# Three products of a recurrent stage rewritten: E by an identity, the decay in one product, the keys' norm by a block of ones

## The chip, the cores and the metric

The kernel runs on one core of one Trainium2 chip. The metric is the device time of one execution in microseconds; shown are the median of three runs and their ends. The program computes a whole network of eight layers in float32; the change touches one stage of it, a recurrent mixer that takes some 700 of its 3980 us.

## The reference, cut to what matters

The stage computes `rwkv_mixer` for 768 time steps (256 of a context, 512 of the sequence) and 16 heads of 64 channels, in two directions:

```python
kk = heads(k * k_k)
kk = kk * lax.rsqrt(jnp.sum(kk * kk, axis=-1, keepdims=True) + 1e-12)      # the keys' norm, per head and step
...
def step(S, inp):
    d_t, k_t, v_t, kk_t, a_t = inp[:5]
    sa = jnp.einsum("bhvk,bhk->bhv", S, -kk_t)
    S = (S * d_t[:, :, None, :] + sa[..., None] * (kk_t * a_t)[:, :, None, :]
         + v_t[..., None] * k_t[:, :, None, :])
    out = jnp.einsum("bhvk,bhk->bhv", S, inp[5])
    return S, out
```

`S` is a 64x64 state for each head, `d_t` the decay of each channel.

## The kernel before

The program is written engine by engine with explicit semaphores: the order of the text is the order on each queue, nothing is reordered. TensorE's products all carry the line of one helper (L1029), ScalarE's functions L1994, and most fused products of VectorE L2589, so the trace is read by tiles and shapes.

**Chunks and groups.** Two heads share the 128 partitions (64 each). There are 8 blocks of two heads (`j`), each with 12 chunks of 64 steps; a group `G` takes 4 chunks in both directions, 8 units in all, so a block is 3 groups (`G % 3` is 0, 1, 2) and there are 24 groups. Inside a chunk the recurrence is a triangular system. Its inverse is built by doubling: E and its transpose F start from the identity (`start_e` L3213, `start_f` L3219 copy the part of a product of features that lies next to the diagonal into it, under a mask) and grow in levels 1 to 5. A level `l` is one round over three engines:

- TensorE `level_z` (L1646; with products of the features of this or the next group in between, L1653): z of 8 units, from `nq` and F
- ScalarE `take_z` (L2372): copies z out of PSUM
- TensorE `level_fz_ez` (L1688): two products a unit, with E (level 5 has only one of the two)
- VectorE `level_f` (L3225) and `level_e` (L3230): copies under a mask; TensorE's next `level_z` waits for `level_f`.

A product of 64x64 is made for each of the two heads, on one quarter of the array each: `heads` (L1504) writes a head's result to its own 64 partitions, `crossed` (L1510) to the other's. One float32 matmul of the program is two weight loads and two products in the trace.

**The chain of states.** Beside the levels of group G the state goes through the 4 chunks of group G-1: `chain_xo` (L1738), `chain_u` (L1759) and `chain_m` (L1765) on TensorE. `chain_m` adds up the new state in PSUM: the old state, multiplied by an identity on each half (`turn`, L1776), and two products. A state step at the first chunk of a block has no old state, the one at the last is left out, so 80 of the 96 steps multiply by the identity.

**E's first product.** `ends(G)` (L1616) is 16 matmuls: features B times features A, crossed, for 8 units, into `qe_ps` (L640), a bank of its own use. It stands in level 3 of the group before, between `chain_xo` and `level_fz_ez` (L1825). `nq` (L2364) is ScalarE's copy of the same features' product, the other way round, made in levels 4 and 5 by `take_b` after VectorE's `mask_b` (L3240).

**The keys' norm.** For block j+1 the work is spread over the levels of block j's first two groups, by the tables `aside` (L1781 for TensorE, L2403 for ScalarE, L3316 for VectorE): ScalarE squares the keys (L2297), TensorE sums the squares of each head for every step, as 6 matmuls with 2 columns of ones (`key_sums` L1519), ScalarE takes the root of 128x12 values (L2316), VectorE its reciprocal (L3190), and TensorE spreads the result over the 64 channels of each head in 12 matmuls (`key_spread` L1528, levels 4 and 5). VectorE multiplies the keys by it out of PSUM in `keys` (L3197): 512 steps in level 4 of the block's first group, 256 in level 1 of its second. GpSimd makes the features A, B, K, R of the block from them (L3609 on); TensorE waits for these features in level 3 of the third group. `read_gains` (L2310, ScalarE) writes the reads' gains into the buffer `bon`, in which the squares stood, and GpSimd goes on from there to the bonus.

**The bonus.** `bonus_sums` (L1540) writes into `spare_ps`, which is the bank of `level_fz_ez`'s first product, in level 5 of each third group; VectorE's `bonus_values` (L3205) reads it behind `level_e`. TensorE waits for that in level 1 of the next group (L1694).

**Before the loop** the rates of all 8 blocks come from matmuls (`lora_up` L1487) whose results ScalarE evicts (`lora_rates` L2289); the keys of block 0 are prepared between those of blocks 1 and 2 (L1796 to L1803, L2433 to L2451).

Of the kernel before, what the change touches and what calls it, by code (L numbers as in the profile page):

```python
# [13 lines left out]
P = 128  # L14
# [150 lines left out]
CHUNK = 64  # L165
# [97 lines left out]
def build(nc, t):  # L263
# [27 lines left out]
    with ExitStack() as ctx:  # L291
# [348 lines left out]
        qe_ps, qt_ps = [lin_ps[:, 0, 512 * i:512 * i + 512].rearrange("p (u t) -> p u t", u=UN) for i in range(2)]  # L640
# [21 lines left out]

        def ends_job(G):

            return 6 * G + 2

        def b_job(G, half):

            return 6 * G + 3 + half

# [356 lines left out]
        def _(pe):  # L1027
# [488 lines left out]
            turn = C("twice")  # L1516
            pe.wait_ge(in_ready, 16 * (LOADS + 2))

            def key_sums(j):  # L1519

                pe.wait_ge(kk_sq, j + 1)
                if j:
                    pe.wait_ge(b_ev, 2 * j)
                for n in range(6):
                    m = mm(pair_ps[:, 2 * n:2 * n + 2], bon[:, n * P:(n + 1) * P], headones[:, 0:P:64], True, True)
                m.then_inc(kk_mm, 1)

            def key_spread(j, part):  # L1528

                if part == 0:  # L1530
                    pe.wait_ge(kk_inv, j + 1)
                else:
                    pe.wait_ge(kk_n, 4 * j + 2)
# [16 lines left out]
            def values(j, part):  # L1550

                if part == 0:
                    pe.wait_ge(value_in, 16 * (j + 1))
                    pe.wait_ge(kk_n, 4 * j + 4)
                else:
                    pe.wait_ge(v_ev, 2 * j + 1)
# [46 lines left out]
            def ready_b(G, half):  # L1603
# [3 lines left out]
                else:  # L1607
                    if G % 3 == 0:
                        pe.wait_ge(read_ready, G // 3 + 1)
                    pe.wait_ge(e_init, G + 1)  # L1610
# [77 lines left out]
            def level_fz_ez(G, l, chain=None):  # L1688

                pe.wait_ge(z_ev, 5 * G + l)  # L1690
                if l == 1:
                    pe.wait_ge(e_init, G + 1)
                    if G and G % 3 == 0:
# [2058 lines left out]
```

## Time and profile before

| | |
|---|---|
| median of 3 runs | 3981.12 us (3980.13 to 3982.87) |
| the profiled execution | 3980.35 us, its span 3978.5 us |
| granted TensorE clock, share | 0.989 |
| TensorE busy | 3769.9 us, 95% of the span |
| weight loads busy | 2778.7 us, 70% |
| VectorE, ScalarE, GpSimd busy | 2301.6, 887.9, 1162.7 us |
| the recurrent loop | 2240 to 2880 us of the span |

The span is the profiled execution from its first to its last instruction; the device time has some 2 us more. The busy time of matmuls is modelled at their ends, so two short products in a row leave no idle time between them though the array is not full. "Idle before" is the time that an engine stood still before a group of its instructions, and behind the arrow stands what ended it; "issue" is the case in which the engine waited for nothing that the profile shows. Times of rows in a timeline are microseconds from the span's start.

### The profile page before, as it was taken

How to read it: one execution, taken by the hardware profiler on the slowest of the kernel's cores; microseconds unless marked ns; L12 is line 12 of the kernel's file. 1: busy time of each engine (PE TensorE's matmuls, PEld its weight loads, DVE VectorE, ACT ScalarE, POOL GpSimd, SP SyncE). 2: the span in 40 equal slices, each digit the busy share in tenths (PEclk: the TensorE clock that was granted, in tenths of full speed). 3: DMA queues.
4: the chain of work that ended last, by engine and by line, in shares of the span. 5: the costliest groups of instructions: out<-in, count | busy, mean ns of one | idle time of the engine just before them, and what ended most of it. 6: DMA issues, size and time to landing. Idle time of an engine off the chain costs nothing.

```text
span 3978.5 us, 77183 instructions
## 1 busy us (share of the span) xinstructions
PE 3769.9 (95%) x33844; PEld 2778.7 (70%) x33844; DVE 2301.6 (58%) x3572; ACT 887.9 (22%) x1689; POOL 1162.7 (29%) x860
## 2 busy tenths in 40 slices
PE   8999999999999999999999788888799999999998
PEld 3588887758888855555555677777757888558445
DVE  4577725658564139934553456655416877662695
ACT  2311101010110020021112544444212222550102
POOL 0154444105445420001341422342013554103202
PEclk9999999999999999999999899999999999999999
DMA  2133223433442211111333411111202333211221
GB/s 80 54 138 139 97 93 125 172 116 128 148 148 85 75 53 50 38 40 64 111 111 103 160 51 45 40 36 36 82 16 77 103 117 97 76 38 56 74 64 53
DMA packets 196056, 336.93 MB, mean 85 GB/s; under 512 B 17040, under 2 KB 149136, under 8 KB 187280
## 3 DMA queue, kind: packets, MB, share of 16 engines
q1 hardware_dynamic: 192000, 321.59, 24.1%
q0 software_dynamic: 3728, 10.49, 1.0%
q8 instruction: 264, 4.33, 0.4%
q14 instruction: 64, 0.52, 0.0%
HBM read 285.91 MB, written 38.80 MB: 82 GB/s over the span
## 4 chain that ended last, share of the span: by engine, by line
PE 86%; DVE 7%; issue 5%; ACT 1%; DMA 1%; SPq 0%; POOL 0%; DVEq 0%; ACTq 0%
PE lin_ps L1029 64%; PE out_ps L1029 8%; PE sum_ps L1029 7%; PE lin_ps L1434 6%; DVE arena L2589 1%; PE sum_ps L1939 1%; DVE rstd L2576 1%; ACT arena L1994 1%; DVE arena L3228 0%; DVE hn L2589 0%; DMA features<-arena 0%; DVE xs L2584 0%; DMA arena<-pos 0%; PE sum_ps L1153 0%; DVE arena L3238 0%
## 5 line engine op out<-in xcount | busy, mean ns | idle before, releaser
L1029 PE MATMUL lin_ps<-hn,ring 128*128 128x256 f32 (+1 forms) x3520 | 1001.0, 441 | 8.2 <-DVE hn L2589 5.1
L1029 PEld LDWEIGHTS lin_ps<-hn,ring 128*128 128x128 f32 x3520 | 667.8, 190 | 316.8 <-issue 249.8
L1029 PE MATMUL lin_ps<-arena 64*64 64x64 f32 (+5 forms) x10032 | 737.7, 261 | 70.5 <-issue 37.3
L1029 PE MATMUL lin_ps<-arena,ring 128*128 128x256 f32 (+1 forms) x3200 | 771.8, 396 | 11.0 <-DVE arena L3057 9.4
L1029 PEld LDWEIGHTS lin_ps<-arena,ring 128*128 128x128 f32 x3200 | 610.2, 191 | 136.3 <-issue 54.3
L1029 PEld LDWEIGHTS lin_ps<-arena 64*64 64x64 f32 (+2 forms) x10032 | 549.8, 145 | 189.9 <-issue 113.8
L2589 DVE SCALAR_TENSOR_TENSOR arena<-arena,vec 128x512 f32<-128x512 f32 (+2 forms) x491 | 384.5, 857 | 1.1
L1994 ACT ACTIVATE arena<-lin_ps 128x512 f32<-128x512 f32 (+3 forms) x375 | 191.7, 525 | 775.9 <-PE lin_ps L1029 707.5
L3544 POOL TENSOR_TENSOR arena<-ring 128x512 f32<-128x512 f32 x67 | 89.8, 1341 | 895.4 <-PE lin_ps L1029 537.9
L1029 PE MATMUL sum_ps<-arena 64*64 64x64 f32 (+1 forms) x7180 | 311.5, 225 | 33.7 <-issue 28.5
L3544 POOL TENSOR_TENSOR ring<-ring 128x512 f32<-128x512 f32 x67 | 102.7, 1533 | 732.0 <-PE lin_ps L1029 428.7
L2589 DVE SCALAR_TENSOR_TENSOR arena<-arena,cs 128x512 f32<-128x512 f32 x280 | 294.8, 1108 | 1.8
L1029 PEld LDWEIGHTS sum_ps<-arena 64*64 64x64 f32 (+1 forms) x7180 | 257.1, 135 | 45.1 <-issue 34.6
L1994 ACT ACTIVATE xs<-lin_ps 128x256 f32<-128x256 f32 x88 | 33.6, 382 | 921.4 <-PE lin_ps L1029 921.4
L1029 PE MATMUL lin_ps<-hn,arena 128*128 128x256 f32 x928 | 214.5, 379 | 0.0
L1029 PEld LDWEIGHTS lin_ps<-hn,arena 128*128 128x128 f32 x928 | 176.3, 190 | 24.0
L1029 PE MATMUL out_ps<-arena 64*64 64x64 f32 (+3 forms) x2142 | 171.3, 254 | 4.4 <-issue 3.2
L2783 DVE TENSOR_TENSOR xs<-lin_ps,xs 128x256 f32<-128x256 f32 x24 | 10.1, 421 | 279.9 <-ACT xs L1994 279.8
L1029 PEld LDWEIGHTS out_ps<-arena 64*64 64x64 f32 (+1 forms) x2142 | 122.7, 143 | 46.4 <-issue 40.0
L1029 PE MATMUL sum_ps<-arena,con 64*64 64x64 f32 (+2 forms) x830 | 129.7, 305 | 21.1 <-ACT arena L1994 16.9
L1994 ACT ACTIVATE arena<-arena 128x512 f32<-128x512 f32 (+3 forms) x220 | 125.4, 626 | 98.6 <-DVE arena L2805 35.3
L3228 DVE COPY_PREDICATED arena<-arena,lin_ps 128x512 f32<-128x512 int32 x96 | 70.3, 732 | 127.2 <-issue 127.1
(279 smaller groups left out, 4918.7 us busy)
## 6 DMA issues: line engine op xcount, KB each, us to landing
ring<-w_up SPq DMA_DIRECT2D x32, 1024.0 KB, 5.9
ring<-w_down SPq DMA_DIRECT2D x32, 1024.0 KB, 5.2
arena<-w_mod SPq DMA_DIRECT2D x24, 1024.0 KB, 7.8
arena<-w_mod SPq DMA_DIRECT2D x12, 2048.0 KB, 7.5
features<-arena SPq DMA_DIRECT2D x64, 384.0 KB, 6.2
ring<-w_conv_in SPq DMA_DIRECT2D x16, 1024.0 KB, 5.7
ring<-w_attn SPq DMA_DIRECT2D x16, 1024.0 KB, 5.8
ring<-features SPq DMA_DIRECT2D x40, 384.0 KB, 3.1
```

The source lines that it names most:

```text
L1029: return pe.matmul(out, lhsT, rhs, start=start, stop=stop)
L1434: m = pe.matmul(wide_bank[bank], w[:, k, :], rhs[:, k, :], start=first and k == 0, stop=k == 3, skip_group_check=not first)
L1939: m = pe.transpose(sum_ps[:, 256 + b * P:256 + (b + 1) * P], probs[U % 3][:, b * P:(b + 1) * P], ident)
L1994: return nc.scalar.activation(out, in_, func, **kw)
L2576: o(nc.vector.reciprocal(last_cols(rstd, width), last_cols(std, width)))
L2589: return nc.vector.scalar_tensor_tensor(*a)
L2783: o(add(c11, quad_ps[0][:, hi_t], p1, ALU.add), ev)
L3228: nc.vector.copy_predicated(by_step(F_[G % 2]), level_mask(l, 1), by_step(fz_ps)).then_inc(f_ready, 1)
L3544: o(tt(s1, a21, a22, ALU.add), block)
```

## The change

Three products of the stage are made in another way, and two of them at another place.

1. E's first product: `ends(G)` is now one `crossed` product over all 8 units, of the identity with `nq` (2 matmuls of 512 columns in place of 16 of 64). It waits for `nq`'s second half, is written into `spare_ps`, and so waits for `bonus_values` where a new block starts. It moves from level 3 of the group before to behind its level 5; `start_e` moves with it on VectorE, behind `level_e` of level 5. The features' products of the next group wait for `f_init` in place of `e_init`.
2. The decay in `chain_m`: one matmul of the 128x128 identity with both directions' old state (128 columns) in place of 4 of 64x64.
3. The keys' norm: TensorE multiplies the squares by a 128x128 block of ones (`headones`), 512 and 256 columns, which gives each channel its head's sum; ScalarE takes the root of all these values into `bon`, VectorE the reciprocal of all of them in `keys`, and multiplies the keys by it out of SBUF. `key_inverse` and `key_spread` are gone. `read_gains` moves from level 1 to level 2 of the second group and waits for the keys.

```diff
+        def b_job(G, half):
+            return 6 * G + 2 + half
         def ends_job(G):
-            return 6 * G + 2
+            return 6 * G + 4
...
-            def key_sums(j):
-                ...
-                for n in range(6):
-                    m = mm(pair_ps[:, 2 * n:2 * n + 2], bon[:, n * P:(n + 1) * P], headones[:, 0:P:64], True, True)
-                m.then_inc(kk_mm, 1)
-            def key_spread(j, part):
...
-                for n in range(4 * part, 4 + 2 * part):
-                    lo = P * (n - 4 * part)
-                    for h, rows in enumerate(HALVES):
-                        m = mm(pair_ps[rows, lo:lo + P], kn[:, 1, 2 * n + h:2 * n + h + 1].to_broadcast([P, CHUNK]), ident, True, True)
-                m.then_inc(kk_bc, 1)
+            def key_sums(j, part):
+                if part:
+                    pe.wait_ge(kk_std, 2 * j + 1)
+                else:
+                    pe.wait_ge(kk_sq, j + 1)
+                    if j:
+                        pe.wait_ge(b_ev, 2 * j)
+                lo, n = (0, 512) if part == 0 else (512, 256)
+                mm(pair_ps[:, 0:n], headones, bon[:, lo:lo + n], True, True).then_inc(kk_mm, 1)
...
-            def end_unit(G, u):
-                b, i, d = G // 3 % 2, chunk_of(G, u // 2, u % 2), u % 2
-                return crossed(qe_ps[:, u, :], fB[b][d][:, i, :], fA[b][d][:, i, :])
...
             def ends(G):
-                for u in range(UN):
-                    m = end_unit(G, u)
-                m.then_inc(gram_mm, 1)
+                pe.wait_ge(gram_act, 6 * G + 3)
+                if G % 3 == 0:
+                    pe.wait_ge(b_ev, 2 * (G // 3) + 1)
+                crossed(spare_ps, turn, flat(nq[G % 2])).then_inc(gram_mm, 1)
...
+                if pos:
+                    mm(flat(m_ps), ident, flat(mst[pos % 2]), True, False)
                 for d in range(2):
                     u, i = 2 * c + d, chunk_of(G, c, d)
-                    if pos:
-                        heads(m_ps[:, d, :], turn, mst[pos % 2][:, d, :], True, False)
...
                 if j + 1 < KD:
-                    if (gg, l) == (0, 1):
-                        key_sums(j + 1)
-                    if (gg, l) in ((0, 4), (0, 5)):
-                        key_spread(j + 1, l // 5)
+                    if (gg, l) in ((0, 1), (0, 3)):
+                        key_sums(j + 1, l // 3)
...
             def read_gains(j):
-                act.wait_ge(kk_mm, j + 1)
+                act.wait_ge(kk_n, 4 * j + 4)
...
-            def key_roots(j):
-                ...
-                f(kn[:, 0, :], pair_ps[:, 0:NCH], ACT.Sqrt, bias=scal(3)).then_inc(kk_std, 1)
+            def key_roots(j, part):
+                act.wait_ge(kk_mm, 2 * j + part + 1)
+                lo, n = (0, 512) if part == 0 else (512, 256)
+                f(bon[:, lo:lo + n], pair_ps[:, 0:n], ACT.Sqrt, bias=scal(3)).then_inc(kk_std, 1)
...
             def keys(j, part):
                 lo, n = (0, 512) if part == 0 else (512, 256)
-                dve.wait_ge(kk_bc, 2 * j + part + 1)
+                dve.wait_ge(kk_std, 2 * j + part + 1)
                 dve.wait_ge(read_ready, j)
-                stt(nkk[:, lo:lo + n], k_[:, lo:lo + n], pder[:, 1, j:j + 1], pair_ps[:, 0:n], ALU.mult, ALU.mult).then_inc(kk_n, 1)
-                stt(kkp[:, lo:lo + n], k_[:, lo:lo + n], par[:, j, 0:1], pair_ps[:, 0:n], ALU.mult, ALU.mult).then_inc(kk_n, 1)
+                o(nc.vector.reciprocal(bon[:, lo:lo + n], bon[:, lo:lo + n]))
+                o.wait()
+                stt(nkk[:, lo:lo + n], k_[:, lo:lo + n], pder[:, 1, j:j + 1], bon[:, lo:lo + n], ALU.mult, ALU.mult).then_inc(kk_n, 1)
+                stt(kkp[:, lo:lo + n], k_[:, lo:lo + n], par[:, j, 0:1], bon[:, lo:lo + n], ALU.mult, ALU.mult).then_inc(kk_n, 1)
```

How the order moves on TensorE. In level 3 before, behind `chain_xo` (rows into `sum_ps` and `out_ps`), the sixteen of E stand ahead of `level_fz_ez` (rows into `lin_ps` and `sum_ps` in turn; `xs` holds half of the features):

```order
L1029 MATMUL sum_ps<-arena,xs 64x64 x2
L1029 MATMUL sum_ps<-arena 64x64 x2
L1029 MATMUL out_ps<-arena,xs 64x64 x2
L1029 MATMUL out_ps<-arena 64x64 x4
L1029 MATMUL lin_ps<-xs 64x64 x16
L1029 MATMUL lin_ps<-arena 64x64 x2
L1029 MATMUL sum_ps<-arena 64x64 x2
L1029 MATMUL lin_ps<-arena 64x64 x2
```

After the change the two of E stand between level 5's one product a unit (the x16 row) and z of the next group's level 1:

```order
L1029 MATMUL out_ps<-arena,xs 64x64 x2
L1029 MATMUL out_ps<-arena 64x64 x4
L1029 MATMUL lin_ps<-xs 64x192 x2
L1029 MATMUL sum_ps<-arena 64x64 x16
L1029 MATMUL lin_ps<-arena,con 64x512 x2
L1029 MATMUL lin_ps<-arena 64x64 x2
L1029 MATMUL lin_ps<-xs 64x192 x2
```

Sixteen rows of work have become two, and they follow level 5 directly.

On VectorE, levels 4 and 5 of a block's first group, before (L3228 and L3233 are `level_f` and `level_e`, L2589 the two products of the keys, L3238 `mask_b`, L3277 the output's sum):

```order
L3228 COPY_PREDICATED arena<-arena,lin_ps 128x512
L3178 MEMSET small 128x1
L3233 COPY_PREDICATED arena<-arena,sum_ps 128x512
L2589 SCALAR_TENSOR_TENSOR ring<-ring,arena,out_ps 128x512 x2
L3238 TENSOR_TENSOR arena<-lin_ps,arena 128x256
L3277 TENSOR_TENSOR arena<-arena,out_ps 128x512
```

and after (L3211, L3216, L2577, L3221, L3260 are the same operations, L3183 is the reciprocal in `keys`, L3200 the start of E):

```order
L3211 COPY_PREDICATED arena<-arena,lin_ps 128x512
L3166 MEMSET small 128x1
L3216 COPY_PREDICATED arena<-arena,sum_ps 128x512
L3183 RECIPROCAL ring<-ring 128x512
L2577 SCALAR_TENSOR_TENSOR ring<-ring,arena 128x512 x2
L3221 TENSOR_TENSOR arena<-lin_ps,arena 128x256
L3260 TENSOR_TENSOR arena<-arena,out_ps 128x512
L3166 MEMSET small 128x1
L3216 COPY_PREDICATED arena<-arena,sum_ps 128x512
L3166 MEMSET small 128x1
L3200 COPY_PREDICATED arena<-arena,lin_ps 128x512
```

The reciprocal of 512 values a partition stands ahead of `mask_b`, and the start of E behind level 5's `level_e`.

On ScalarE, before the loop, the roots of block 0 before:

```order
L1994 ACTIVATE ring<-arena 128x768 x2
L1994 ACT_TABLE_LOAD
L1994 ACTIVATE arena<-out_ps,con 128x12
L1994 ACT_TABLE_LOAD
L1994 ACTIVATE arena<-rstd 128x12x64
```

and after:

```order
L1980 ACTIVATE ring<-arena 128x768 x2
L1980 ACT_TABLE_LOAD
L1980 ACTIVATE ring<-out_ps,con 128x512
L1980 ACTIVATE ring<-out_ps,con 128x256
L1980 ACT_TABLE_LOAD
L1980 ACTIVATE arena<-rstd 128x12x64
```

Two roots over all values stand in the place of one over 12, with as many table loads as before.

## Rows read from the trace of the kernel before

**Rows 1.** The page's busy times: TensorE.
```profile
PE 3769.9 (95%) x33844; PEld 2778.7 (70%) x33844; DVE 2301.6 (58%) x3572; ACT 887.9 (22%) x1689; POOL 1162.7 (29%) x860
```

**Rows 2.** Windows, levels 1 to 5 of group 10: us, then PE, PEld, DVE, ACT, POOL busy.
```profile
2499.39:2503.72 4.33, 3.67 (x158) 3.13 (x155) 3.33 (x10) 3.45 (x10) 4.01 (x3) 1.00 0.04 8
2503.72:2508.64 4.92, 4.92 (x202) 4.66 (x204) 4.92 (x11) 2.68 (x7) 4.58 (x3) 1.00 0.01 3
2508.64:2515.60 6.96, 5.23 (x245) 4.77 (x240) 3.04 (x10) 2.47 (x6) 6.66 (x4) 1.00 0.02 5
2515.60:2521.16 5.56, 4.86 (x195) 4.39 (x196) 3.43 (x9) 3.13 (x7) 5.33 (x4) 1.00 0.01 3
2521.16:2524.71 3.55, 3.35 (x116) 3.14 (x112) 3.48 (x6) 1.25 (x4) 3.39 (x3) 1.00 0.02 5
```

**Rows 3.** Waits, 2240 to 2880 us: us in total, times, longest.
```profile
PE lin_ps L1029 <- issue: 42.7, 57, 1.7
PE sum_ps L1029 <- issue: 33.3, 34, 3.3
PE lin_ps L1029 <- DVE arena L3211: 2.8, 7, 0.4
```

**Rows 4.** DMA queues, 2240 to 2880 us: packets, MB, share of 16 engines.
```profile
q8 instruction: 163, 2.67, 1.7%
```

**Rows 5.** TensorE's timeline in group 1: start, us, what, idle before.
```profile
2273.87 0.27 PE L1029 MATMUL lin_ps<-xs 64*64 64x64 f32 x1 [1.20 <-issue]
2277.71 0.27 PE L1029 MATMUL lin_ps<-arena 64*64 64x64 f32 x2 [0.58 <-issue]
```

**Rows 6.** ScalarE's and TensorE's timelines, level 3 of group 10.
```profile
2510.70 0.60 ACT L1994 ACTIVATE arena<-lin_ps 128x512 f32<-128x512 f32 x1 [1.11 <-PE lin_ps L1029]
...
2511.20 0.92 PE L1029 MATMUL lin_ps<-arena 64*64 64x64 f32 x25
...
2511.95 0.28 PE L1029 MATMUL lin_ps<-arena 64*64 64x64 f32 x3
```

**Rows 7.** TensorE's timeline, bonus sums behind the features' products in level 5.
```profile
2390.36 0.49 PE L1029 MATMUL lin_ps<-xs 64*64 64x192 f32 x3
2390.78 1.12 PE L1029 MATMUL lin_ps<-ring,con 128*128 128x512 f32 x2
2391.74 0.59 PE L1029 MATMUL out_ps<-ring,con 128*128 128x256 f32 x2
```

**Rows 8.** VectorE's timeline, groups 9 (levels 4, 5) and 10 (levels 1, 2).
```profile
2496.12 1.38 DVE L2589 SCALAR_TENSOR_TENSOR ring<-ring,arena,out_ps 128x512 f32<-128x512 f32 x2
2498.16 0.42 DVE L3238 TENSOR_TENSOR arena<-lin_ps,arena 128x256 f32<-128x256 f32 x1 [0.66 <-PE lin_ps L1029]
...
2504.39 2.08 DVE L3290 TENSOR_TENSOR arena<-arena 128x768 f32<-128x768 f32 x1
...
2507.85 0.74 DVE L3228 COPY_PREDICATED arena<-arena,lin_ps 128x512 f32<-128x512 int32 x1
```

**Rows 9.** Groups by line and shape, VectorE's reciprocals: count, busy, mean ns.
```profile
L2576 DVE RECIPROCAL rstd<-std 128x512 f32<-128x512 f32 x8 | 26.8, 3350 | 24.1 <-ACT std L1994 24.1
L2576 DVE RECIPROCAL rstd<-std 128x768 f32<-128x768 f32 x4 | 19.8, 4953 | 32.2 <-ACT std L1994 32.2
```

**Rows 10.** VectorE's timeline at the end of group 5.
```profile
2393.47 0.74 DVE L3233 COPY_PREDICATED arena<-arena,sum_ps 128x512 f32<-128x512 int32 x1 [1.56 <-issue]
...
2394.10 0.67 DVE L3211 TENSOR_TENSOR arena<-lin_ps,ring 128x512 f32<-128x512 f32 x1
```

**Rows 11.** Timeline of all engines ahead of the loop.
```profile
2193.98 0.27 ACT L1994 ACTIVATE arena<-out_ps,con 128x12 f32<-128x12 f32 x1
...
2197.41 1.40 DVE L2589 SCALAR_TENSOR_TENSOR ring<-ring,arena,out_ps 128x512 f32<-128x512 f32 x2
...
2199.17 0.92 ACT L1994 ACTIVATE ring<-ring,arena 128x768 f32<-128x768 f32 x1
...
2202.35 1.22 PE L1029 MATMUL sum_ps<-arena 64*128 64x256 f32 x2 [2.36 <-ACT arena L1994]
```

More of the change, by code:

```diff
@@ L638, in by_dir @@
             return v.rearrange("p (d t) -> p d t", d=2)
-        qe_ps, qt_ps = [lin_ps[:, 0, 512 * i:512 * i + 512].rearrange("p (u t) -> p u t", u=UN) for i in range(2)]
+        qt_ps = lin_ps[:, 0, 512:1024].rearrange("p (u t) -> p u t", u=UN)
         gram_ps = lin_ps[:, 0, :].rearrange("p (c r) -> p c r", c=2)[:, :, 0:6 * CHUNK]
@@ L661, in turned_ends_job @@
             return 6 * G + 1
+        def b_job(G, half):
+            return 6 * G + 2 + half
         def ends_job(G):
-            return 6 * G + 2
-        def b_job(G, half):
-            return 6 * G + 3 + half
+            return 6 * G + 4
         def k_job(G, half):
@@ L1516, in _, with flat @@
             turn = C("twice")
+            def flat(v):
+                return v.rearrange("p a t -> p (a t)")
             pe.wait_ge(in_ready, 16 * (LOADS + 2))
-            def key_sums(j):
-                pe.wait_ge(kk_sq, j + 1)
-                if j:
-                    pe.wait_ge(b_ev, 2 * j)
-                for n in range(6):
-                    m = mm(pair_ps[:, 2 * n:2 * n + 2], bon[:, n * P:(n + 1) * P], headones[:, 0:P:64], True, True)
-                m.then_inc(kk_mm, 1)
-            def key_spread(j, part):
-                if part == 0:
-                    pe.wait_ge(kk_inv, j + 1)
-                else:
-                    pe.wait_ge(kk_n, 4 * j + 2)
-                for n in range(4 * part, 4 + 2 * part):
-                    lo = P * (n - 4 * part)
-                    for h, rows in enumerate(HALVES):
-                        m = mm(pair_ps[rows, lo:lo + P], kn[:, 1, 2 * n + h:2 * n + h + 1].to_broadcast([P, CHUNK]), ident, True, True)
-                m.then_inc(kk_bc, 1)
+            def key_sums(j, part):
+                if part:
+                    pe.wait_ge(kk_std, 2 * j + 1)
+                else:
+                    pe.wait_ge(kk_sq, j + 1)
[3 more added lines that the diff above has]
+                mm(pair_ps[:, 0:n], headones, bon[:, lo:lo + n], True, True).then_inc(kk_mm, 1)
             def bonus_sums(j):
@@ L1553, in values @@
                     pe.wait_ge(value_in, 16 * (j + 1))
-                    pe.wait_ge(kk_n, 4 * j + 4)
+                    pe.wait_ge(kk_std, 2 * j + 2)
                 else:
@@ L1692, in level_fz_ez @@
                     pe.wait_ge(e_init, G + 1)
-                    if G and G % 3 == 0:
-                        pe.wait_ge(b_ev, 2 * (G // 3) + 1)
                 pe.wait_ge(e_ready, 5 * G + l - 1)
@@ L1796, in _ @@
             lora_up(range(0, 11))
-            key_sums(0)
             for part in range(2):
-                key_spread(0, part)
+                key_sums(0, part)
             lora_up(range(11, 20))
@@ L1807, in _ @@
             turned_ends(0)
-            ends(0)
             for half in range(2):
@@ L1811, in _ @@
                 features(0, 0, half)
+            ends(0)
             for G in range(GROUPS):
@@ L1824, in _ @@
                         chain_xo(G - 1, l - 1)
-                    if l == 3 and not last:
-                        ends(G + 1)
                     level_fz_ez(G, l, chain=G)
@@ L1837, in _ @@
                 level_fz_ez(G, 5)
+                if not last:
+                    ends(G + 1)
             G = GROUPS - 1
@@ L2411, in aside @@
                     if (gg, l) == (0, 2):
-                        key_roots(j + 1)
+                        key_roots(j + 1, 0)
                         key_gains(j + 1, 0)
@@ L2416, in aside @@
                     if (gg, l) == (0, 4):
+                        key_roots(j + 1, 1)
                         decays(j + 1, 0)
@@ L2421, in aside @@
                         decay_ends(j + 1)
+                    if (gg, l) == (1, 2):
                         read_gains(j + 1)
@@ L2440, in _ @@
             key_gains(0, 1)
-            key_roots(0)
+            for part in range(2):
+                key_roots(0, part)
             for d in range(2):
@@ L3373, in _ @@
                 mask_b(0, half)
+            start_e(0)
             for G in range(GROUPS):
@@ L3392, in _ @@
                         bonus_values(G // 3 + 1, 0)
+                    if l == 5 and not last:
+                        start_e(G + 1)
                     aside(G, l)
```

19 lines of the change are left out of this document (3 added, 16 removed).

## The prediction

> **What bounds the kernel now.** The page first: TensorE is busy 95% of the span [rows 1], so the time is lost or won on its queue. But in the recurrent loop (2240 to 2880 us, 24 groups of five levels) this is not plain arithmetic. One group, cut at the start of each level's first product, takes 4.3, 4.9, 7.0, 5.6 and 3.6 us [rows 2]. Levels 3 and 4 have 1.7 and 0.7 us with no product in flight, and they are also the ones with most instructions: counts of PE and PEld together are 485 and 391, against 313, 406 and 228. The waits say what ends that idle time [rows 3]: not ScalarE, not VectorE, but "issue", 76 us on the two largest tiles. The queues name a candidate: 163 instruction packets in these 640 us, 2.67 MB, so 16 KB or 256 instructions of 64 bytes each, one every 3.9 us [rows 4]. And the stalls stand in step with it: two of them end at 2273.87 and 2277.71, 3.84 us apart, one 1.20 and one 0.58 us long, in the middle of a run of products that wait for nothing [rows 5]. So I read: **TensorE gets 256 instructions in some 3.7 us and no faster**; whoever needs them sooner stands still. A program's float32 matmul is four of them (two weight loads, two products: where the order shows 16, the trace has 32). Levels 1, 2 and 5 are bound otherwise, by the round of products, ScalarE's copy and VectorE's masked copy.
>
> **What the change does, part by part.** Places: 23 groups start inside the loop (the first before it), 7 of the 8 key blocks are prepared inside it, 80 state steps have a decay product.
>
> 1. Instructions. Removed in the loop: 14 matmuls for E in 23 groups, 3 in each of 80 decay products, 16 in each of 7 key norms: 674 matmuls, 2,696 instructions, 10.5 packets. Of these 64 a group leave level 3, some 39 decay steps (12 each) lie in levels 3 and 4, and 28 a key block leave them: 2,136 instructions or 8.3 packets. At 3.7 us a packet that is **-31 us**. In these two levels nothing else that the change does counts, since the supply ends last. The ends: 10.5 packets times 3.7 is -39; if a packet's edge only costs its mean stall (76 us over 163 packets, 0.5), -5. I take the first because stall and distance fit it [rows 2, 5].
>
> 2. E by an identity. Today its sixteen products stand in level 3 between the last ones of the chain and the next `level_fz_ez`: 25 of their 32 records take 0.92 us, so all take about 0.93, and the following products start at 2511.95, though the copy that they need is through at 2511.30 [rows 6]: 0.5 of the 0.93 is not hidden. That gain falls in level 3 and is in term 1 already. Now two products of 512 columns stand behind level 5, where nothing hides them. The nearest row is a full 128x512 product, 0.96 us to the next one's start [rows 7]; the two halves use disjoint parts of the array, as pairs do today. I take 0.8 (0.9 less the overlap at the edges), one after the other it would be 1.7. 23 x 0.8 = **+18**. VectorE's masked copy for E moves from level 3, where VectorE idles, behind level 5's; the products of the next level 1 and their copy (2 us) cover its 0.75. Without that cover `level_fz_ez` of level 1 would start up to 0.75 late.
>
> 3. E's product writes the bank that the bonus sums use, so in 7 groups TensorE must now wait for `bonus_values` before it. VectorE does `level_e` from 2393.47 and the bonus from 2394.10 for 0.67 [rows 10]; before, the next level's products started some 0.45 before that `level_e`. Now they wait until 2394.8: 1.8 us, x7 = 12.7, less the 2.8 us that level 1 waits for the same result now [rows 3]: **+10**. Behind TensorE's wait stand E, z and all of the next group.
>
> 4. Decay. Two pairs of 64x64 products (0.23 us) become one 128x128 of 128 columns, some 0.21 of streaming by the 128x512 row. But it needs the whole array between products on quarters: before the 128x512 row the quarters' last ones must drain, and it starts 0.25 after the last of them [rows 7]. Cost between -0.02 and +0.4; the wait for the masked copy behind it hides about 0.25. I take +0.1 and count the 41 steps outside levels 3 and 4: **+4**.
>
> 5. The 512-wide part of the key norm. A reciprocal of 128x512 takes 3.35 us, of 768 4.95, so 1.6 to 1.75 for 256 [rows 9]; today it is 12 wide. It stands on VectorE in level 4 of each block's first group. `level_e` starts 0.63 before what follows it [rows 10], so here at 2495.5. From there: 0.63, 3.35, two keys' products 1.38, then `mask_b` 0.42 [rows 8], ScalarE's copy 0.4 and two hand-overs 0.1: TensorE may go on at +6.3, where today level 1 starts at +3.9 (the row of level 1 in rows 2 starts at 2499.39). +2.4, x7 = **+17**. ScalarE's Sqrt of the other 256 and the removed spread products lie inside this.
>
> 6. The 256-wide part stands in level 1 of the second group, where VectorE runs without a gap from 2504.39 to the masked copy that TensorE's level 3 awaits [rows 8]: all of 1.75 shows, x7 = **+12**. `read_gains` (0.93 on ScalarE) moves to the same place's level 2 and makes the next copy 0.2 late: **+1**. GpSimd waits for it some 6 us longer. That is hidden today by some 13 us: it works to the end of this group, the last two products (4 us) are no features, and the features are wanted two levels (9 us) into the next [rows 2]. Without this cover all of the 6 would show, seven times.
>
> 7. Before the loop. ScalarE's `read_gains(0)` now waits for the keys, and behind it on ScalarE stand the rates' evictions, for which TensorE waits at 2202.35. The roots are Sqrt over 512 and 256 (0.60 + 0.38 in place of 0.27) with a product and two hand-overs between: some 1.9 later for the decays, and so the keys begin at 2199.3 in place of 2197.41. Then 3.35 + 1.38 + 1.75 + 0.8 = 7.3, so `read_gains` starts near 2207 in place of 2199.17 [rows 11]: **+8**. Ends 6 and 9.5.
>
> 8. What is made late gives the supply time. Levels 3 and 4 hold 2.4 us of stall a group [rows 2], 58 of the 76; the other 18 lie in levels 1, 2 and 5, and a packet that lands during an added wait is no stall afterwards. Half of them and a little more: **-10** (0 to -18).
>
> Sum: -31 + 18 + 10 + 4 + 17 + 12 + 1 + 8 - 10 = +29. The profiled execution took 3980.35 us (span 3978.5), the median is 3981.12, 0.8 above: 3980.4 + 29 = 4009.4, on the median's footing **4010 us**. SP's and GpSimd's order is unchanged.
>
> The Trainium skill (Runtime: NRT & Kernel Launch, section Instruction fetch mechanics) says that the stream is refilled in blocks of 16 KiB and that crossing a block's edge costs "one DMA tail-bump, mostly hidden". The packets' size agrees with it [rows 4]; that it is mostly hidden does not, with stalls of 1.20 and 0.58 us at two edges in a row [rows 5]. By the page terms 1 and 8 would be near nought, which is the first rival below.
>
> **The rivals.**
> - *An edge costs a fixed stall, the supply is no rate.* Then the packets that are gone return 0.5 each, -5, level 3 gains E's 0.5 x 23 = -12, the decay costs +4 more in levels 3 and 4, and nothing is absorbed: 70 - 5 - 12 + 4 = +57 on the added terms' 70, **4038**. For it: the stalls differ in length (0.58, 1.20). Against: they are longest where the products are densest.
> - *Quarter products do not overlap as hoped*: the two halves of E run one behind the other (+0.8 x 23) and the switch to the whole array costs 0.3 (+0.2 x 41): +26 on the forecast, **4036**. For it: the order has all of one half's pieces ahead of the other's. Against: pairs overlap today in that order.
> - *Not slower: the supply bounds all five levels once the stalls move.* Place: from level 5's end to level 2. If E's 0.8 and half of each VectorE wait fall where the next packet is still under way, they cost nothing: -39 for 10.5 packets, 18 and about 17 of the 41 of waits absorbed: 70 - 39 - 18 - 17 = -4, **3977 to 3985**. It decides when levels 1 and 5 need more than 3.7 us a packet's worth without the additions; today level 1 has 313 instructions in 4.3 us [rows 2], which is 3.5 us a packet, near it. Against: there the idle time is not issue.
> - *The change misses its purpose elsewhere*: GpSimd's features get late (the 14 us are used up) and TensorE waits for them in level 3: **4030 to 4050**.
>
> **How the numbers follow.** A measurement of this kernel tells 0.2% (8 us) from no change. Chances: forecast 0.57, fixed stall 0.12, no overlap 0.11, supply everywhere 0.17, GpSimd 0.03. The forecast's own terms span about 3990 to 4030 (prologue 2 either way, term 8 from 0 to -18, decay +0.2 x 41); for 8 in 10 the range goes to 3986 below, where half of the not-slower case is, and to 4036 above. Faster by over 0.2% (under 3973) 0.08, within 0.2% (to 3989) 0.12, slower 0.80.
>
> **What would show it.** In the profile after: instruction packets in the loop down by about ten; level 3 of a group near 5.8 us in place of 7.0, with its issue time less than half; two 64x512 products of some 0.9 us together behind each level 5; TensorE standing 2 us or more for VectorE in level 5 of each block's first group and 1.7 in level 2 of the second; 1.8 us for `bonus_values` seven times; the rates' evictions starting near 2209. Wrong would be: level 3 still 7.0 us (the supply is no rate), E's products at 1.7, or reciprocals that fall in time that VectorE has free.

## The result, and the profile after

The changed kernel takes **4014.22 us** (median of 4 runs, 4014.14 to 4018.72) against 3981.99 us (4 runs, 3980.13 to 3984.82): ratio 1.0085, 95% interval 1.0069 to 1.0101, slower by 32 us. The forecast was 4010, plus 29. The profiled execution is the 4018.72 one (span 4016.8), 38.4 above that of before; so the pair of traces shows some 6 us more than the medians do.

The page's busy times and its queue of instructions, after (that queue had 264 packets before):

```profile
PE 3779.4 (94%) x32436; PEld 2762.4 (69%) x32436; DVE 2343.9 (58%) x3580; ACT 894.3 (22%) x1697; POOL 1165.2 (29%) x860
...
q8 instruction: 253, 4.15, 0.4%
```

1,408 products fewer, and TensorE is busy 10 us longer than in [rows 1]: a busy share says little here. The stretches that answer to [rows 2] are level 5 of group 9 with E's product, and levels 1 to 5 of group 10 (columns as there; the three last figures are the granted clock, the DMA share, GB/s):

```profile
2521.95:2530.54 8.59, 4.25 (x114) 3.45 (x116) 8.34 (x8) 3.46 (x7) 6.06 (x3) 0.99 0.01 3
2530.54:2535.66 5.12, 4.78 (x142) 4.12 (x139) 3.84 (x10) 2.93 (x8) 3.63 (x2) 0.69 0.03 6
2535.66:2541.23 5.57, 5.29 (x202) 4.86 (x202) 5.54 (x12) 1.84 (x6) 0.00 (x0) 1.00 0.01 3
2541.23:2546.87 5.64, 4.38 (x192) 3.92 (x194) 2.30 (x8) 3.20 (x7) 4.29 (x3) 1.00 0.02 6
2546.87:2551.62 4.75, 4.75 (x198) 4.41 (x196) 3.11 (x8) 2.40 (x4) 4.59 (x3) 1.00 0.01 3
2551.62:2555.79 4.17, 3.60 (x118) 3.22 (x114) 3.62 (x7) 1.92 (x7) 4.01 (x3) 1.00 0.01 4
```

Level 3 has gone from 6.96 to 5.64 us and level 4 from 5.56 to 4.75. But level 5 of the group before is 8.59, where the kernel before had 3.5 (2495.88 to 2499.39), and level 1 ran at a mean clock of 0.69. TensorE's waits, 2250 to 2925 us (us in total, times, longest):

```profile
PE lin_ps L1029 <- ACT arena L1980: 35.7, 36, 4.3
PE sum_ps L1029 <- issue: 26.7, 31, 1.6
PE lin_ps L1029 <- issue: 22.1, 30, 3.1
...
PE lin_ps L1029 <- DVE arena L3194: 10.4, 7, 1.5
```

Issue on the two tiles fell from 76 us [rows 3] to 49. In its place TensorE stands 36 us for ScalarE's copy (9.7 before), up to 4.3 at a time, and 10.4 for `bonus_values` (L3194 is L3211 of before, 2.8 us there).

The whole loop in one table; each run in it is described under The experiments. A level is measured from the end of one z to the end of the next, by the semaphore events of the trace; means over groups 1 to 22, one profiled execution each. Level 5 therefore holds E's product and the next z.

```
kernel           level 1    2     3     4     5   group   median us   ratio to before (95%)
before              5.05  5.50  7.11  5.56  4.08  27.29
the change          4.97  5.20  6.25  5.35  6.62  28.40    4014.22    1.0085 (1.0069-1.0101)
e_only              5.20  5.29  5.94  5.71  5.30  27.44    3981.20    0.9999 (0.9989-1.0009)
decay_only          5.17  5.06  6.83  5.63  4.03  26.73    3962.66    0.9954 (0.9937-0.9970)
decay_again         5.04  5.18  6.81  5.46  3.97  26.46    3964.15    0.9955 (0.9942-0.9968)
norm_only           4.91  5.54  7.01  5.46  5.37  28.29    4019.36    1.0093 (1.0076-1.0110)
one_wide            4.98  5.54  7.22  5.56  4.00  27.29    3976.88    0.9995 (0.9985-1.0005)
many_tiny           5.29  5.44  8.07  5.63  3.96  28.38    3994.75    1.0029 (1.0019-1.0038)
gpsimd_waits        4.90  5.66  5.93  5.32  6.04  27.84    4002.58    1.0051 (1.0034-1.0069)
filled_wait         4.89  5.20  6.09  5.37  6.48  28.03    4008.10    1.0068 (1.0049-1.0087)
bonus_first         4.89  5.28  6.17  5.40  6.16  27.90    4007.11    1.0058 (1.0037-1.0079)
three_repairs       4.84  5.49  5.88  5.38  5.40  26.98    3984.74    1.0007 (0.9998-1.0017)
ends_in_five        5.54  5.16  5.81  5.74  4.51  26.77    3965.73    0.9959 (0.9946-0.9972)
e_decay_bonus       5.08  5.08  5.74  5.78  4.59  26.27    3957.93    0.9933 (0.9914-0.9951)
```

From one profiled execution to another the start of the loop moves by some 5 us in the same code, so the loop is compared by this table and the kernel by its median. In the change, levels 1 to 4 lose 1.45 us a group, over these 22 groups 32 us, and level 5 gains 2.54, 56 us. The loop starts 7.3 later, and group 0, which the means leave out, is 7.1 longer: 56 - 32 + 7 + 7 = 38, which is the difference of the two profiled executions.

What level 5 of group 9 is made of. VectorE's timeline (start, us, what):

```profile
2521.74 0.73 DVE L3216 COPY_PREDICATED arena<-arena,sum_ps 128x512 f32<-128x512 int32 x1
...
2522.37 3.33 DVE L3183 RECIPROCAL ring<-ring 128x512 f32<-128x512 f32 x1
2525.74 2.96 DVE L2577 SCALAR_TENSOR_TENSOR ring<-ring,arena 128x512 f32<-128x512 f32 x2
2528.62 0.41 DVE L3221 TENSOR_TENSOR arena<-lin_ps,arena 128x256 f32<-128x256 f32 x1
```

GpSimd's, in the same microseconds:

```profile
2525.99 2.16 POOL L3603 TENSOR_TENSOR xs<-ring,rstd 128x768 f32<-128x768 f32 x1
2528.29 2.09 POOL L3600 TENSOR_TENSOR ring<-ring 128x768 f32<-128x768 f32 x1
```

And TensorE behind it, its timeline and then two windows:

```profile
2529.50 0.65 PE L1029 MATMUL lin_ps<-arena,con 64*64 64x512 f32 x2 [4.30 <-ACT arena L1980]
```

```profile
2525.00:2529.40 4.40, 0.20 (x8) 0.06 (x2) 4.36 (x5) 0.34 (x2) 4.11 (x3) 1.00 0.00 0
2531.00:2533.00 2.00, 2.00 (x48) 1.68 (x44) 1.97 (x3) 0.75 (x2) 1.59 (x1) 0.50 0.03 8
```

The chain is the forecast's: `level_e`, reciprocal, two products of the keys, `mask_b`, ScalarE's copy, TensorE. Two things in it are not. The two products take 2.96 us where the trace of before had 1.38 [rows 8]: the first ends in 0.75; the second takes 2.29, and a multiplication of GpSimd had begun 0.4 before it. And after 4.3 us without a product TensorE's granted clock is 0.50, its lower level of 1.2 GHz, when E and z come.

### The profile page after: what moved, and what is told of

Same layout as the page of the kernel before. It is cut to its first block and busy times, and to the rows that moved or that the text cites. A ratio compares the mean times of both kernels' runs of the same rounds, so it can differ in the third digit from the quotient of the medians.

```text
span 4016.8 us, 74370 instructions
## 1 busy us (share of the span) xinstructions
PE 3779.4 (94%) x32436; PEld 2762.4 (69%) x32436; DVE 2343.9 (58%) x3580; ACT 894.3 (22%) x1697; POOL 1165.2 (29%) x860
## 5 line engine op out<-in xcount | busy, mean ns | idle before, releaser
L1029 PE MATMUL lin_ps<-arena 64*64 64x64 f32 (+5 forms) x9648 | 728.9, 264 | 60.4 <-issue 22.4
L2577 DVE SCALAR_TENSOR_TENSOR arena<-arena,vec 128x512 f32<-128x512 f32 (+2 forms) x491 | 384.5, 858 | 1.1
L1029 PE MATMUL sum_ps<-arena 64*64 64x64 f32 (+1 forms) x7180 | 302.4, 226 | 49.2 <-issue 24.5
L1029 PEld LDWEIGHTS sum_ps<-arena 64*64 64x64 f32 (+1 forms) x7180 | 247.1, 136 | 72.5 <-issue 30.4
L2577 DVE SCALAR_TENSOR_TENSOR arena<-arena,cs 128x512 f32<-128x512 f32 x280 | 295.6, 1111 | 1.8
L3211 DVE COPY_PREDICATED arena<-arena,lin_ps 128x512 f32<-128x512 int32 x96 | 69.9, 729 | 141.9 <-issue 141.9
L3541 POOL TENSOR_TENSOR hn<-hn 128x512 f32<-128x512 f32 (+1 forms) x16 | 23.5, 1467 | 402.5 <-ACT hn L1980 401.5
```

The lines of the kernel that those rows point to most:

```text
L1029: return pe.matmul(out, lhsT, rhs, start=start, stop=stop)
L2577: return nc.vector.scalar_tensor_tensor(*a)
L3211: nc.vector.copy_predicated(by_step(F_[G % 2]), level_mask(l, 1), by_step(fz_ps)).then_inc(f_ready, 1)
L3541: o(nc.gpsimd.tensor_tensor(a, a, last_cols(dst[:, k, :], width), ALU.add), partial if k == last else None)
```

## The experiments

**1. The three parts apart.** `e_only`, `decay_only` and `norm_only` are the kernel before with one numbered part of the change each, nothing else.

> Of the three parts only E's: the identity product behind level 5, start_e with it; decay and keys' norm as before. If TensorE's instructions come at a rate (3.7 us for 256), 56 fewer of them a group in level 3 give back 19 us, E's products behind level 5 cost 12 to 18 and the wait for bonus_values 10 to 12: 3982 to 3992 us. If a packet's edge costs a fixed stall, little comes back (12 to 14 with the work itself) and the time is 3992 to 3998.

> Of the three parts only the decay's: one 128x128 product for four of 64x64. Rate: 12 fewer instructions in each of 39 steps of levels 3 and 4 give back 7 us, the switch to the whole array costs 0 to 4: 3975 to 3980. Fixed stall or a dear switch: 3984 to 3992.

> Of the three parts only the keys' norm. By the trace of the change this is where the loss sits: TensorE stands for nq's second half in level 5 of each block's first group, 5 us more than before (reciprocal 3.3, the second product of the keys 1.5 longer, then products at half clock), seven times 5.2 = 36; before the loop 7; the 256-wide part 2; less 4 for the instructions that go: 4018 to 4026. If E's product behind that wait is what makes it so long (its queue, its clock), the norm alone costs the 25 of the forecast's terms and no more: 4002 to 4010.

Measured: E 3981.20, no difference (1 us under the rate's range); decay 3962.66, 17.6 less than before, far more than either theory gave; norm 4019.36, 39 more, in the range that put the loss here. So the change is a loss of one part, a gain of another and one that comes to nothing. Their sum is some +22, and the change costs 32. A gap of 10 us between four medians lies within their intervals, but the table has it too: levels 1 to 4 of the parts are 1.08 (E), 0.53 or 0.73 (decay, two measurements) and 0.30 us (norm) shorter than before, 1.9 or 2.1 together, and those of the change 1.45. What the parts give back there doesn't add up.

In `e_only` level 5 grows by 0.69 us in the first and second groups of a block: E's two products. In the changed kernel, at full clock (TensorE, from 2555.79), each of the two rows into 64x512 below holds both halves, which start 7 ns apart; the second row follows the first at 0.48, and z starts at their heels:

```profile
2555.79 0.65 PE L1029 MATMUL lin_ps<-arena,con 64*64 64x512 f32 x2
2556.07 0.38 PE L1029 MATMUL lin_ps<-arena 64*64 64x192 f32 x2
2556.27 0.60 PE L1029 MATMUL lin_ps<-arena,con 64*64 64x512 f32 x2
2556.28 1.56 PE L1029 MATMUL lin_ps<-arena 64*64 64x192 f32 x42
```

In the third groups it grows by 2.37. Levels 1 to 4 give back 1.30, 1.02 and 0.54 a group by its place in the block (groups 0 to 22), 22 us in all, for 1,288 instructions (5.0 packets, 18.6 us at 3.7).

**2. Is it the count of instructions, or the work?** `one_wide` (the first diff) and `many_tiny` are the kernel before with something superfluous ahead of `ends(G + 1)` in level 3, into a bank that E's sixteen then overwrite:

```diff
                     if l == 3 and not last:
+                        mm(qe_ps.rearrange("p a t -> p (a t)"), ident, nq[G % 2].rearrange("p a t -> p (a t)"), True, True)
                         ends(G + 1)
```

```diff
                     if l == 3 and not last:
+                        for u in range(UN):
+                            crossed(qe_ps[:, u, 0:1], turn, nq[G % 2][:, u, 0:1])
                         ends(G + 1)
```

> The kernel before with one product too many in level 3 of each of 23 groups, 128x128 by 512 columns, 4 instructions and 0.96 us of the array, into the bank that E's sixteen then overwrite. Rate: the array stands 1.7 us in level 3 waiting for instructions, so 0.96 us of work with 4 instructions falls into that and costs 23 x 4/256 x 3.7 = 1.3 us and a bit at the edges: 3982 to 3989. If the stalls are fixed and TensorE's work is what bounds level 3, all of 0.96 shows, 23 times: 4000 to 4004.

> The kernel before with 16 products too many in level 3 of each of 23 groups, 64x64 by one column, 64 instructions. The one wide product (4 instructions, 0.96 us of the array) cost nothing there. Rate: 23 x 64/256 x 3.7 = 21 us more, 3998 to 4003, though they stream a 64th of what E's sixteen do. If work and not the count is what costs, under half of that: 3981 to 3991.

Windows over level 3 of group 13, of before, `one_wide` and `many_tiny`, a fence each:

```profile
2588.92:2595.78 6.86, 5.18 (x236) 4.73 (x232) 3.03 (x10) 2.49 (x6) 6.56 (x4) 1.00 0.02 5
```

```profile
2589.70:2596.09 6.39, 6.36 (x246) 5.21 (x242) 2.50 (x10) 1.97 (x5) 6.09 (x4) 1.00 0.02 5
```

```profile
2600.82:2609.28 8.46, 6.18 (x278) 5.77 (x274) 2.28 (x8) 1.54 (x4) 8.00 (x6) 1.00 0.02 4
```

In `one_wide` TensorE was busy 1.2 us longer in a level that became no longer, with this among its products:

```profile
2591.65 1.12 PE L1029 MATMUL lin_ps<-arena,con 128*128 128x512 f32 x2
```

Over all groups its level 3 is 0.11 longer (7.22 for 7.11), and the kernel is not slower (0.9995). Sixteen products of one column make level 3 0.96 longer: 64 instructions are a quarter of a packet, 0.92 at 3.7 us. A wide product is free and tiny ones cost: **TensorE is held by the number of its instructions.** The median of `many_tiny` rose by 13 only, between the two ranges of its expectation (16 to 21, or under 10), where its profiled loop shows 22 x 1.09 = 24. It ran between 3989 and 4000, and the profiled execution was the longest of the ten: which way it goes is firm, the total is not.

The trace of before shows the packets themselves. With TensorE's instructions in order (weight loads, products and its sequencer's waits), 125 times in groups 1 to 22 more than 0.45 us pass from one start to the next, and 100 of these stand at the same place of 256. These 154 places carry 113 us in all; in `one_wide` they carry 80, so the superfluous product went into the stalls. And 69 of the 78 stretches of over 0.5 us in which TensorE neither loads nor multiplies end 1.1 to 1.5 us after a 16 KB packet has landed, after which the next packet starts 1.15 later and takes 1.05 (medians). 1.4 + 1.15 + 1.05 is 3.6, near the 3.77 that lie between two packets (median): the rate looks like one packet's way after the other, not like a width. That is read from the trace and was not tested by a run.

**3. The second product of the keys.** The changed kernel with one wait on GpSimd:

```diff
                 pool.wait_ge(o_mm, max(3 * j - 3, 0))
+                if j:
+                    pool.wait_ge(kk_n, 4 * j + 2)
```

> The changed kernel, and GpSimd begins a block's features only after the two 512-wide products of the keys (for blocks 1 to 7). Theory: the second of them takes 2.28 us in place of 0.74 because both of its large operands are in SBUF and GpSimd is in a multiplication of its own at that time. Then it takes 0.75, TensorE's wait in level 5 of a block's first group is 1.5 us shorter, seven times: 11 us less than the change's 4014, 4000 to 4007, unless GpSimd's later work meets VectorE elsewhere. Rival: the second product is slow for a reason of its own (its operands' places, the reciprocal's writes): it stays at 2.28 and the time at 4014.

Three lines of VectorE's groups by line and shape, 2240 to 2900 us (count | busy, mean ns | idle before), of the change:

```profile
L2577 DVE SCALAR_TENSOR_TENSOR ring<-ring,arena 128x512 f32<-128x512 f32 x14 | 21.3, 1560 | 0.2
...
L3273 DVE TENSOR_TENSOR arena<-arena 128x768 f32<-128x768 f32 x7 | 6.6, 945 | 0.0
L2577 DVE SCALAR_TENSOR_TENSOR ring<-ring,arena 128x256 f32<-128x256 f32 x14 | 6.2, 481 | 0.2
```

and the same of `gpsimd_waits`:

```profile
L3273 DVE TENSOR_TENSOR arena<-arena 128x768 f32<-128x768 f32 x7 | 13.2, 1886 | 0.0
L2577 DVE SCALAR_TENSOR_TENSOR ring<-ring,arena 128x512 f32<-128x512 f32 x14 | 9.9, 749 | 0.2
L2577 DVE SCALAR_TENSOR_TENSOR ring<-ring,arena 128x256 f32<-128x256 f32 x14 | 7.6, 582 | 0.2
```

The 512-wide products are back at 749 ns and the kernel at 4002.58, 11.6 less, as expected; TensorE's wait is 2.78 us in place of 4.30 in group 9. VectorE stood still for GpSimd. (Part of the 11.6 is the clock's, see 4.) The same rows show it elsewhere: L3273 is `out_center` in level 1 of a block's second group, both operands in SBUF. It took 2.08 us in [rows 8], beside GpSimd; in the changed kernel GpSimd stands idle there, waiting for `read_gains`, and it takes 0.95; where GpSimd works on (here), 1.89, and level 2 of these groups is 0.78 us longer again. The Trainium skill (SBUF — State Buffer, section SBUF: two separate sides) has the rule: a VectorE instruction with two inputs in SBUF and a GpSimd instruction that reads SBUF share a port pair, and whoever starts first keeps it to the end. The trace agrees: in `gpsimd_waits` the same product, with nothing of GpSimd beside it, is back at 0.75. Before, one input of the keys' products was in PSUM, and they did not pay. In the loop none of the 512-wide ones fell beside GpSimd, but those of block 0 did [rows 11] and took 0.74 each, beside this:

```profile
2197.36 1.82 POOL L3622 TENSOR_TENSOR xs<-ring,rstd 128x768 f32<-128x768 f32 x1 [3.69 <-ACT rstd L1994]
```

The 256-wide ones took 0.47 beside GpSimd in every block. Moved to SBUF, the 512-wide ones of block 0 take 0.86 and 2.28.

**4. The clock.** The changed kernel with superfluous work in TensorE's wait:

```diff
                 level_fz_ez(G, 5)
+                if G % 3 == 0 and not last:
+                    for n in range(3):
+                        mm(flat(z_ps), ident, flat(nq[G % 2]), True, True)
```

> The changed kernel with three products of 128x128 by 512 columns too many, 2.9 us, into z's bank while TensorE stands in level 5 of each block's first group. If the fall of the granted clock to 1.2 GHz for 3 us behind that wait costs what the trace suggests (products of 64x64 at 0.31 in place of 0.22), it doesn't fall, E and z take 1.0 less, seven times: 4005 to 4010. If the clock costs nothing there because VectorE or ScalarE end last, or if it falls all the same, 4012 to 4018.

TensorE's timeline at the end of group 9 there:

```profile
2518.13 2.84 PE L1029 MATMUL lin_ps<-arena,con 128*128 128x512 f32 x6
2521.17 0.65 PE L1029 MATMUL lin_ps<-arena,con 64*64 64x512 f32 x2 [0.19 <-ACT arena L1983]
...
2521.65 0.60 PE L1029 MATMUL lin_ps<-arena,con 64*64 64x512 f32 x2
```

4008.10, 6.1 less with more work (by the intervals of the two ratios, not clear of noise). In six of the seven blocks the 4 us around the end of z now have a granted clock of 1.00 (0.59 in the one left); in the change they have 0.50 to 0.82 in all seven. Level 5 of the first groups is 0.69 shorter, as a mean of eight. But that mean hides the clock's price: the eighth first group has no keys to prepare and so no wait, and the three products cost it 2.3 us; the block whose clock fell all the same lost 1.0. In the six blocks whose clock stayed, level 5 is 1.5 shorter (0.95 to 1.70). `gpsimd_waits` says the same without any added product. There the clock stays at 1.00 in four blocks and falls in three; one of each (4 us around the end of z, columns as in [rows 2], then the clock):

```profile
2603.67:2607.67 4.00, 3.60 (x134) 2.90 (x134) 3.34 (x9) 2.83 (x7) 3.71 (x3) 1.00 0.02 4
2689.36:2693.36 4.00, 3.66 (x128) 3.34 (x124) 2.52 (x6) 1.30 (x5) 3.69 (x3) 0.76 0.02 4
```

Its level 5 is 3.1 us longer than before in those four and 4.7 in the three. So a fall of the clock behind this wait costs about 1.5 us, an estimate from two runs.

**5. The bonus wait.** The changed kernel with `bonus_values(G // 3 + 1, 0)` ahead of `level_e(G, l)` on VectorE, where it had 1.56 us free [rows 10].

> The changed kernel with VectorE's first bonus_values ahead of level_e in level 5 of a block's third group, in time that VectorE has free. The wait that E's product got costs 1.7 us more than E itself in these groups (2.3 against 0.7 in the other groups); without it 7 x 1.6: 4001 to 4006. If level 5 of the third group is long for another reason (the bonus products, level_e later), 4012 to 4016.

4007.11, 7.1 less, 1 us over the range; level 5 of the third groups is 1.79 shorter, 12.5 us over seven, and the wait for L3194 is gone from the list. The median fell by less than that, with runs from 3999.9 to 4010.3, and by the intervals it is not clear of the change's.

**6. What is left, and a better kernel.** `three_repairs` is the changed kernel with 3, 4 (two products in place of three) and 5. `ends_in_five` has the decay's part and E's sixteen products of 64x64, not the identity, in level 5 ahead of `level_fz_ez`, where TensorE waits for the copy of z (behind it in third groups); on VectorE `bonus_values` goes ahead of `level_e` too. `e_decay_bonus` is parts 1 and 2 with `bonus_values` first and the old keys' norm. `decay_again` is `decay_only` on the same chip.

```diff
 # ends_in_five, against the change's part 1
             def ends(G):
-                pe.wait_ge(gram_act, 6 * G + 3)
...
-                crossed(spare_ps, turn, flat(nq[G % 2])).then_inc(gram_mm, 1)
+                for u in range(UN):
+                    m = end_unit(G, u)
+                m.then_inc(gram_mm, 1)
...
                 aside(G, 5)
+                if not last and G % 3 < 2:
+                    ends(G + 1)
                 level_fz_ez(G, 5)
-                if not last:
+                if not last and G % 3 == 2:
                     ends(G + 1)
```

> The changed kernel with all of: GpSimd waiting for the 512-wide keys, bonus_values first, two products of 512 columns in TensorE's wait. One by one they gave 11, 7 and 6 less than 4014. If they are three mechanisms they add up but for what filling is worth in a wait that is already shorter: 3988 to 3996, still slower than before, by what reciprocals, the prologue and E's products cost. If they overlap: 4000.

> The decay's part, and E's sixteen products of 64x64 as before but in level 5, in the time in which TensorE waits for ScalarE's copy of z (in each third group behind level_fz_ez), with start_e and bonus_values ahead of level_e. If the supply of instructions ends last in levels 3 and 4 alone, moving 64 instructions a group out of level 3 saves 0.9 there and costs 0.2 to 0.5 in level 5: 3950 to 3955. If it bounds the loop as a whole (the decay alone gave back 3.7 us for each of its packets wherever they lay), a move saves nothing: 3961 to 3966.

> E's part and the decay's of the change, the keys' norm as before, and bonus_values ahead of level_e. E alone was worth nothing (its instructions back, its products and the bonus wait paid), the decay alone 17 less than before, the bonus wait 7 to 12. With what each packet less returns falling off as the supply stops being what ends last: 3955 to 3962, some 20 to 26 less than before and at or under the decay alone. If the waits of VectorE and ScalarE bound the loop once the decay's instructions are gone: as the decay alone, 3963.

> The decay's part alone once more, beside the two above on one chip: 3960 to 3966, 14 to 20 less than the kernel before, as 960 instructions in the loop are 3.75 packets of 3.7 us. If the first measurement was a lucky one: 3971 to 3980.

`three_repairs` is at 3984.74, no longer slower than before (0.9998 to 1.0017) and 3 us under what was expected: one by one they gave 11.6, 6.1 and 7.1, 25 in all, and together 29: they add up within the noise (its ten runs lie between 3978.9 and 3992.0) and are nearly the whole loss. `ends_in_five` is the decay alone, not better (3965.73 and 3964.15): a level 3 at 5.81 is paid back in levels 1 and 5, as the rival had it. Moving instructions is worth nothing, dropping them is. `e_decay_bonus`, with 56 a group fewer still and the bonus wait gone, has the lowest median, **3957.93 us**, 0.9933 (0.9914 to 0.9951), 23 us under the kernel before. That it beats the decay alone, by 6 us, is not shown: the two intervals overlap, and its six runs lie between 3946 and 3966.

## Why the prediction was right

The direction and the size held (29 forecast, 32 measured), partly by luck: errors cancelled.

- **Supply (terms 1 and 8, forecast -31 and -10).** The mechanism is shown, with its price: 0.92 expected for 64 instructions and 0.96 measured, while 0.96 us of the array cost 0.11. Levels 1 to 4 returned 32, a sum of supply and of the small costs that fall there. The gaps at every 256th instruction, groups 1 to 22, sum to 113 us over 154 edges before and 77 over 144 after: ten packets fewer, as forecast.
- **A step that failed in term 1: "some 39 decay steps lie in levels 3 and 4", the rest left uncounted.** The decay's part alone gave 17.6 and 16.7 us (its interval in the second measurement is 13 to 23) where this working has -7 + 4. All 80 steps are 960 instructions, 3.75 packets, 14 us: the supply bounds the loop as a whole, and level 2 (5.50 to 5.06 and 5.18) is shortened as level 3 is. `ends_in_five` says the same. That was half of the rival "the supply bounds all five levels", to which I gave 0.17. It was right that instructions count outside levels 3 and 4 too, and wrong that E's product and the waits then cost nothing: 0.69 of E's 0.8 shows. Whether a shorter `chain_m` itself gives some of the decay's gain was not tried apart. In the change the parts' gains overlap: 22 for E, some 14 for the decay and 7 for the norm come to 32.
- **Decay (term 4, +4).** No cost of the switch to the whole array can be seen in a part that gains more than its packets; -0.02, the low end, was the better value.
- **E (term 2, +18).** 0.69 in place of 0.8 for its two products: 16. As forecast, halves side by side, not 1.7.
- **Bonus (term 3, +10).** 1.7 more than E in each third group of `e_only`, 12; the wait itself 10.4 less 2.8.
- **The 512-wide norm (term 5, +17).** The term that was mis-sized. In `norm_only` level 5 of the seven first groups that have it is 5.2 longer, 36. To the forecast's 2.4 a block come 1.5 more for the second product, for which "two keys' products 1.38 [rows 8]" was taken from a form with an operand in PSUM, and about 1.5 for the clock (4), which the forecast did not have at all. 2.4 + 1.5 + 1.5 is 5.4 for the 5.2.
- **The 256-wide norm (term 6, +12).** Hardly there: `norm_only` has +0.48 in level 1 and -0.30 in level 2 of these groups. "VectorE runs without a gap, all of 1.75 shows" overlooked that part of what filled it was `out_center` waiting for GpSimd, which the change stops. The change's timeline in group 10 has 0.96, 1.76 and `level_f` in time:

```profile
2536.32 0.96 DVE L3273 TENSOR_TENSOR arena<-arena 128x768 f32<-128x768 f32 x1
2537.19 1.76 DVE L3183 RECIPROCAL ring<-ring 128x256 f32<-128x256 f32 x1
...
2540.45 0.73 DVE L3211 COPY_PREDICATED arena<-arena,lin_ps 128x512 f32<-128x512 int32 x1
```

- **`read_gains` and GpSimd (in term 6, +1).** GpSimd waits 7.2 us for `read_gains` in group 10, and TensorE never for GpSimd in the change's list of waits: hidden, as forecast.
- **Before the loop (term 7, +8).** In the two traces ScalarE's `read_gains` starts at 2206.46 for 2199.17, and TensorE's next product at 2209.66 for 2202.35 [rows 11]: 7.3. That is luck of this pair. The squares of block 0, which a DMA releases, began 2.2 us earlier in the change's profiled execution. From them on it is 9.5: the keys begin 2.2 later (forecast 1.9), and from there to `read_gains` it takes 9.07 in place of 1.75 in all six kernels with the new norm (forecast 7.3 for the 9.07), because here too the second product takes 2.28 beside GpSimd.

```profile
2206.46 0.93 ACT L1980 ACTIVATE ring<-ring,arena 128x768 f32<-128x768 f32 x1 [7.22 <-DVE ring L2577]
```

```profile
2209.66 1.22 PE L1029 MATMUL sum_ps<-arena 64*128 64x256 f32 x2 [15.94 <-ACT arena L1980]
```

Where the terms fall, in the profiled pair: level 5 (terms 2, 3 and 5, forecast 45) grew by 63 with group 0, 19 of the miss in term 5. Levels 1 to 4 (terms 1, 4, 6 and 8, forecast -24) came to -32, because 11 of term 6 and the 4 of term 4 did not come, while the supply gave some 7 less than its 41. The forecast is thus 9 us short of the pair's 38, and 3 short of the medians' 32. One statement ahead of the prediction is wrong: `qe_ps` is not a bank of its own use, the features' products (`gram_ps`) use the same one in turn. Nothing in the sum hung on it.

## What to carry to other kernels

Where a stretch is full of small matmuls, count instructions before work: look whether the idle time called "issue" comes at every 256th instruction and what a packet takes, and then merge products, even into ones that stream more, rather than move them. When an operand moves from PSUM to SBUF (or back), ask again what VectorE's instruction shares with GpSimd at that moment; its duration from a trace holds for its operands' places only. A long wait of TensorE costs more than its length where the clock falls behind it (here 1.5 us more), and superfluous work in the wait can be cheaper than silence, but only where the wait is: where there was none, it cost 2.3.

## What was not expected of the hardware

- A VectorE product of 128x512 with two operands in SBUF took 0.75 us, and 2.29 when a GpSimd multiplication of 2.1 us had begun 0.4 before it; a 128x768 one 0.95, and 1.80 to 2.60 beside GpSimd (11 of 12, `before` and `gpsimd_waits`; the twelfth, 0.98, met the last 0.2 of a multiplication). With one operand in PSUM a 128x512 one took 0.74 beside GpSimd (block 0) and without.
- After 4.3 us without a product the granted clock was 0.50 for the next 2 us or more (1.2 GHz in place of 2.4); it fell in all seven blocks. With the wait at about 2.8 us (`gpsimd_waits`) it fell in three of the seven, and level 5 was 1.6 us longer in these.
- 256 TensorE instructions arrive in some 3.7 to 3.9 us: 154 packets in the 600 us of groups 1 to 22, 3.77 from one to the next (median). One superfluous 128x512 product in each of 23 groups is free (3976.88 against 3980.22).
